# Feed-forward block of a streaming encoder layer: Strassen's seven products for eight, gate/up and down as two parts

## What is computed

```python
h = rms(x, ln1)
x = x + concat[SSD, HGRN2, FoX, RG-LRU](h @ w_in) @ w_out
h2 = rms(x, ln2)
x = x + (silu(h2 @ w_gate) * (h2 @ w_up)) @ w_down
```

## Time and profile before

| | |
|---|---|
| median of the runs shown | 2912.92 us |
| fastest run | 2911.31 us |
| profiled execution, span from first to last instruction | 2911.2 us |
| TensorE matmuls | 2832.2 us busy, 97% of the span |
| VectorE, ScalarE, GpSimd busy | 769.9, 820.2, 1010.4 us |
| phase 1 / w_out / feed-forward, by the trace | up to about 995 / 1199 / 2902 us |

### The profile page before, as it was taken

How to read it: one execution, slowest core, us unless ns; L and a number is a source line. 1 busy time by engine, 2 the same in 40 slices (tenths; PEclk the granted TensorE clock), 3 DMA queues, 4 the chain that set the end, 5 groups by cost and what they waited for, 6 DMA issues and landing times.

```text
span 2911.2 us, 47529 instructions
## 1 busy us (share of the span) xinstructions
PE 2832.2 (97%) x20795; PEld 2763.5 (95%) x20795; DVE 769.9 (26%) x1178; ACT 820.2 (28%) x1107; POOL 1010.4 (35%) x439
## 2 busy tenths in 40 slices
PE   5899999999999999999999999999999999999999
PEld 5899999988888999999999999999999999999998
DVE  6835444411125522311111111121111111111112
ACT  4333544443344522411212121211112121212121
POOL 3623222222223343333333333333333333333331
PEclk8999999999999999999999999999999999999999
DMA  6222222222223432323222222222232222222322
GB/s 196 75 74 75 68 66 79 68 71 71 71 56 117 126 94 80 87 76 84 87 73 88 78 83 88 73 87 85 76 88 84 77 87 73 87 78 83 87 79 89
DMA packets 372941, 244.86 MB, mean 84 GB/s; under 512 B 13024, under 2 KB 339916, under 8 KB 372172
## 3 DMA queue, kind: packets, MB, share of 16 engines
q1 hardware_dynamic: 356116, 228.55, 27.5%
q10 hardware_dynamic: 16632, 13.31, 1.5%
HBM read 225.40 MB, written 16.44 MB: 83 GB/s over the span
## 4 chain that ended last, share of the span: by engine, by line
PE 91%; DVE 6%; ACT 2%; issue 1%; DMA 0%; SPq 0%; ACTq 0%; POOL 0%; DVEq 0%
PE pair L546 89%; DVE scratch L1381 1%; ACT scratch L936 1%; DVE scratch L1373 1%; ACT L936 1%; DVE h_lo L1373 1%; DVE xtok L1381 1%; PE pair L755 1%; PE pair L577 0%; DVE scratch L1377 0%; DVE scratch L1378 0%; DMA xtok<-in_x_prompt_dram 0%; PE pair L922 0%; DVE y L1373 0%; DVE xT L1373 0%
## 5 line engine op out<-in xcount | busy, mean ns | idle before, releaser
L491 POOL TENSOR_TENSOR w_lo<-raw,w_hi 128x1024 fp32r<-128x1024 f32 x402 | 976.7, 2431 | 1852.7 <-ACT w_hi L936 1851.9
L546 PE MATMUL pair<-h_hi,w_hi 128*128 128x288 f32 x5024 | 1090.2, 299 | 33.7 <-DVE h_lo L1373 20.0
L546 PE MATMUL pair<-h_hi,w_lo 128*128 128x288 f32 x5024 | 1077.5, 296 | 0.0
L546 PE MATMUL pair<-h_lo,w_hi 128*128 128x288 f32 x5024 | 1077.3, 296 | 0.0
L546 PEld LDWEIGHTS pair<-h_hi,w_hi 128*128 128x128 f32 x5024 | 810.5, 189 | 43.6 <-issue 17.7
L546 PEld LDWEIGHTS pair<-h_lo,w_hi 128*128 128x128 f32 x5024 | 811.4, 189 | 0.0
L546 PEld LDWEIGHTS pair<-h_hi,w_lo 128*128 128x128 f32 x5024 | 811.3, 189 | 0.0
L936 ACT ACTIVATE w_hi<-raw 128x1024 fp32r<-128x1024 f32 x402 | 423.3, 1055 | 1017.5 <-PE pair L546 973.5
L546 PE MATMUL pair<-act_hi,w_hi 128*128 128x288 f32 x1408 | 304.7, 298 | 0.0
L546 PE MATMUL pair<-act_lo,w_hi 128*128 128x288 f32 x1408 | 302.6, 296 | 0.0
L546 PE MATMUL pair<-act_hi,w_lo 128*128 128x288 f32 x1408 | 302.6, 296 | 0.0
(11 more groups left out here) (179 smaller groups left out, 1102.6 us busy)
## 6 DMA issues: line engine op xcount, KB each, us to landing
raw<-in_w_in_dram SPq DMA_DIRECT2D x52, 1024.0 KB, 5.6
raw<-in_w_gate_dram SPq DMA_DIRECT2D x44, 1024.0 KB, 5.6
raw<-in_w_up_dram SPq DMA_DIRECT2D x44, 1024.0 KB, 5.6
raw<-in_w_down_dram SPq DMA_DIRECT2D x44, 1024.0 KB, 5.0
raw<-in_w_out_dram SPq DMA_DIRECT2D x16, 1024.0 KB, 6.0
xT_spill<-xT SPq DMA_DIRECT2D x4, 1152.0 KB, 10.1
xT<-xT_spill SPq DMA_DIRECT2D x4, 1152.0 KB, 10.5
xtok<-in_x_prompt_dram SPq DMA_DIRECT2D x4, 1024.0 KB, 7.4
```

The source lines that it names most:

```text
L491: pool.tensor_tensor(lo, src, hi.bitcast(F32), ALU.subtract).then_inc(S["lo_done"], 1)
L546: return nc.tensor.matmul(out, lhsT, rhs, start=start, stop=stop)
```

## The change

The feed-forward block is written anew with Strassen's scheme in Winograd's form. The matrices are cut in two along rows, along columns and along the tokens, and 7 products of quarters take the place of 8.

**Gate and up.** The weight quarters are gate and up of one feature tile for k-tiles 0 to 7 and for 8 to 15; the activation quarters are the token halves of the same k-tiles. A unit `u` is one feature tile, 44 of them (UG). Each of its 7 products is 8 k-tiles times 3 terms, 24 matmuls of 288 columns, all into one PSUM bank. The results are taken out of four banks (X, Y, Z, W) and added up on the way.

**Down.** The 44 tiles of the activations are 22 pairs, in 5 chunks of 5, 5, 4, 4, 4 pairs (CHUNK_PAIRS). A unit is two output tiles of one chunk, 8 units a chunk (UD), 40 in all. A product is 5 or 4 pairs times 3 terms: 15 or 12 matmuls.

**Weights.** VectorE makes four combinations of a unit's weight quarters (`combine`), each of 128 x 1024 for gate and up, 128 x 640 or 128 x 512 for down. ScalarE makes the seven `f_hi`. `f_lo` of products 0 and 5 is made by GpSimd (POOL_LO), of the other five by VectorE (DVE_LO). The buffers form a ring of three, `hi_ahead(s)` and `lo_ahead(s)` make those of product s+2 while product s runs. Weights are loaded two units ahead (`next_unit`).

**Activations.** The RMS factor is now applied before the split: `x_slot` on VectorE scales x by ln2 and `rstd2`, makes the four activation combinations and all seven `lo` within unit 0, and TensorE's product p of unit 0 waits for them (`in_lo`). Each even and odd unit's silu(gate) * up give a pair, GpSimd makes its four combinations (`combine_glu`), and SyncE writes the seven to DRAM (`spill_glu`, 5 DMAs). For each chunk of down the seven come back, one `load_stage` per product into two buffers `stage`, and are split again (`d_hi_slot` on ScalarE, `d_lo_slot` on VectorE) while the last unit of the chunk before runs.

**Residual.** x goes to DRAM tile by tile during w_out (`spill_x`) and comes back in 8 DMAs after the last gate/up product. The loops of the w_out and feed-forward phases are written out. Phase 1 keeps its instructions; some buffers lie at other addresses. The last 5 of 20 output transposes come after the last product, the other 15 between products of the last chunk.

```diff
+UG = FF // P
+CHUNK_PAIRS = (5, 5, 4, 4, 4)
+CHUNK_AT = (0, 5, 10, 14, 18)
+NC = len(CHUNK_PAIRS)
+UD = KT // 2
+U_ALL = UG + NC * UD
+LAST_C = U_ALL - UD
+PRODUCTS = 7 * U_ALL
+POOL_LO = (0, 5)
+DVE_LO = (1, 2, 3, 4, 6)
...
+            def next_unit(u):
+                sp.wait_ge(S["lo_by_pool"], 2 * u + 2)
+                sp.wait_ge(S["lo_by_dve"], 5 * u + 5)
+                if u + 2 < U_ALL:
+                    load_unit(u + 2)
...
+            def load_stage(c, p):
+                i, j0, n = 7 * c + p, CHUNK_AT[c], CHUNK_PAIRS[c]
+                sp.wait_ge(S["glu_spilled"], 80 * (j0 + n))
+                if i >= 2:
+                    sp.wait_ge(S["in_lo"], 14 + i - 1)
+                sp.dma_start(stage[i % 2][:, 0:n, :], glu_dram[j0:j0 + n, p].rearrange("j p n -> p j n")
+                             ).then_inc(S[f"stage{i % 2}_loaded"], 16)
...
+            for u in range(U_ALL):
+                c = chunk_after(u)
+                if c is None:
+                    next_unit(u)
+                else:
+                    for p in range(5):
+                        load_stage(c, p)
+                    next_unit(u)
+                    load_stage(c, 5)
+                    load_stage(c, 6)
+                if u < UG and u % 2 == 1:
+                    spill_glu(u // 2)
+                if u == UG - 1:
+                    sp.wait_ge(S["f_used"], 7 * UG)
+                    for m in range(KT // 2):
+                        sp.dma_start(xT[m // 4][:, 2 * m % 8:2 * m % 8 + 2, :],
+                                     xT_dram[2 * m:2 * m + 2].rearrange("k p t -> p k t")
+                                     ).then_inc(S[f"x_loaded{X_BACK[m][0]}"], 16)
...
+            def lo_ahead(s):
+                u, p = divmod(s + 2, 7)
+                if p in POOL_LO and u < U_ALL:
+                    pool.wait_ge(S["f_hi_done"], s + 3)
+                    slot = (s + 2) % 3
+                    pool.tensor_tensor(tiles(f_lo[slot], u), source(u, p), tiles(f_hi[slot], u).bitcast(F32),
+                                       ALU.subtract).then_inc(S["lo_by_pool"], 1)
...
+            for s in range(-2, PRODUCTS):
+                lo_ahead(s)
+                u, p = divmod(s, 7)
+                if p == 1 and 2 <= u <= UG and u % 2 == 0:
+                    combine_glu(u // 2 - 1)
...
-                            for r, (w, x) in enumerate(((wh, act_hi), (wh, act_lo), (wl, act_hi))):
-                                for b in range(2):
-                                    c0 = k * 2 * P + jj * P
-                                    m = mm(dst[:, b * 512:b * 512 + HT], w[:, c0:c0 + P],
-                                           x[:, k, b * HT:(b + 1) * HT], k == 0 and r == 0, k == 3 and r == 2)
...
+                if p == 4:
+                    pe.wait_ge(S["u_evac"], 5 * u + 2)
+                elif p == 5:
+                    pe.wait_ge(S["p1_ready"], u + 1)
+                elif p == 6:
+                    pe.wait_ge(S["u_evac"], 5 * u + 3)
...
+                wh, wl, dst = f_hi[s % 3], f_lo[s % 3], psum_of(u, BANK_OF[p])
+                for j in range(n):
+                    if u == 0 and j % 4 == 0:
+                        pe.wait_ge(S["in_lo"], 2 * p + j // 4 + 1)
+                    for q, (w, x) in enumerate(((wh, x_hi), (wh, x_lo), (wl, x_hi))):
+                        m = mm(dst, w[:, j * P:(j + 1) * P], x[:, j, :], p < 4 and j == 0 and q == 0,
+                               j == n - 1 and q == 2, skip_group_check=p > 3)
+                m.then_inc(S["f_used"], 1)
...
+            def hi_ahead(s):
+                u, p = divmod(s + 2, 7)
+                if u >= U_ALL:
+                    return
+                if p in (1, 2, 3, 4):
+                    act.wait_ge(S["s_made"], 4 * u + {1: 2, 2: 1, 3: 3, 4: 4}[p])
+                else:
+                    act.wait_ge(S[f"f_raw{u % 2}_loaded"], 32 * (u // 2 + 1))
+                if s + 2 >= 3:
+                    act.wait_ge(S["f_used"], s)
+                own.tell(fn(tiles(f_hi[(s + 2) % 3], u), source(u, p), ACT.Copy), "f_hi_done")
...
+            def d_hi_slot(c, p, u):
+                i, n = 7 * c + p, CHUNK_PAIRS[c]
+                act.wait_ge(S[f"stage{i % 2}_loaded"], 16 * (i // 2 + 1))
+                act.wait_ge(S["f_used"], 7 * u + p + 1)
+                own.tell(fn(dx_hi[p][:, 0:n, :], stage[i % 2][:, 0:n, :], ACT.Copy), "in_hi")
...
+                if which == 0:
+                    dve.wait_ge(S[f"f_raw{u % 2}_loaded"], 32 * (u // 2 + 1))
+                    own.tell(tt(source(u, 2), quadrant(u, 1, 0), quadrant(u, 1, 1), ALU.add), "s_made")
+                elif which == 1:
+                    dve.wait_ge(S["s_made"], 4 * u + 1)
+                    own.tell(tt(source(u, 1), source(u, 2), quadrant(u, 0, 0), ALU.subtract), "s_made")
+                elif which == 2:
+                    own.tell(tt(source(u, 3), quadrant(u, 0, 0), quadrant(u, 1, 0), ALU.subtract), "s_made")
+                else:
+                    dve.wait_ge(S["s_made"], 4 * u + 2)
+                    own.tell(tt(source(u, 4), quadrant(u, 0, 1), source(u, 1), ALU.subtract), "s_made")
+            def lo_ahead(s):
+                u, p = divmod(s + 2, 7)
+                if p in DVE_LO and 0 <= u < U_ALL:
+                    dve.wait_ge(S["f_hi_done"], s + 3)
+                    slot = (s + 2) % 3
+                    own.tell(tt(tiles(f_lo[slot], u), source(u, p), tiles(f_hi[slot], u).bitcast(F32), ALU.subtract),
+                             "lo_by_dve")
...
+            def x_slot(p):
+                t1, t2, t3 = gx_t[:, 4], gx_t[:, 0], gx_t[:, 3]
+                if p == 0:
+                    dve.wait_ge(S["rstd_ready"], 2)
+                    dve.wait_ge(S["xt_spilled"], 64 + 16 * KT)
+                    x_scaled(B11, 0)
+                    x_lo_slot(0, xq[:, B11])
+                elif p == 1:
+                    x_scaled(B12, 0)
+                    dve.wait_ge(S["x_made"], 16)
+                    x_combined(t1, xq[:, B12], xq[:, B11])
+                    x_scaled(B22, 8)
+                    dve.wait_ge(S["x_made"], 26)
+                    x_combined(t2, xq[:, B22], t1)
+                    x_lo_slot(1, t2)
...
+            def d_lo_slot(c, p):
+                i, n = 7 * c + p, CHUNK_PAIRS[c]
+                dve.wait_ge(S["in_hi"], 14 + i + 1)
+                own.tell(tt(dx_lo[p][:, 0:n, :], stage[i % 2][:, 0:n, :], dx_hi[p][:, 0:n, :].bitcast(F32), ALU.subtract),
+                         "in_lo")
+            def take(u, p, dst, x):
+                dve.wait_ge(S["f_used"], 7 * u + p + 1)
+                own.tell(tt(dst, x, psum_of(u, BANK_OF[p]), ALU.add), "u_evac")
...
+            def step(s):
+                if s > 0:
+                    u, p = divmod(s - 1, 7)
+                    evacuate_unit(u, p)
+                u, p = divmod(s, 7)
+                if p in (3, 4, 5):
+                    if u + 1 < U_ALL:
+                        combine(u + 1, p - 3)
+                elif p == 1:
+                    combine(u, 3)
+                lo_ahead(s)
+                if s > 0:
+                    u, p = divmod(s - 1, 7)
+                    if chunk_after(u) is not None:
+                        d_lo_slot(chunk_after(u), p)
...
```

More of the change, by code:

```diff
@@ L248, in hybrid_layer, with psum_of @@
+        def psum_of(u, which):
+            t = pair[2 * banks_of(u) + which // 2]
+            return t[:, 512 * (which % 2):512 * (which % 2) + HT]
+        X, Y, Z, W = range(4)
+        BANK_OF = (X, Y, Z, W, Z, X, W)
         C_BIAS, C_SGN, C_A, C_LS8, C_NLS8, C_LB, C_1MLB, C_NM, C_RS, C_RI, C_T, C_QN, C_SD = (
@@ L459, in _ @@
[L459 to L474 removed]
+            sp.wait_ge(S["norm_lo"], KT)
@@ L931, in _ @@
+            for c in range(5):
+                out_step(3, c)
         @block.scalar
@@ L1884, in _, with add_residual @@
-            swiglu(0, True)
-            with dve.Fori(1, GROUPS - 1) as g:
-                swiglu(g, False)
-            swiglu(GROUPS - 1, False, True)
+            def add_residual(k):
+                dve.wait_ge(S["half_used"], 2 * k + 2 * N1 + 2)
+                own.tell(tt(x_tile(k), x_tile(k), banks(pair[(k + 3) % 4]), ALU.add), "x2_done")
+                dve.wait_ge(S["x2_squared"], k + 1)
+                if k > 0:
+                    dve.wait_ge(S["x2_summed"], k)
+                own.tell(tt(ss2[:, :], ss2[:, :], sq2[k % 2][:, :], ALU.add), "x2_summed")
@@ new lines, in lo_ahead, with x_scaled @@
+            def lo_ahead(s):
[5 more added lines that the diff above has]
+                             "lo_by_dve")
+            def x_scaled(q, k0):
+                t = q in (B12, B22)
+                for j in range(8):
+                    own.tell(stt(xq[:, q, j, :], xq[:, q, j, :], pcol[:, R_LN2 + k0 + j:R_LN2 + k0 + j + 1],
+                                 rstd2[:, t * HT:(t + 1) * HT], ALU.mult, ALU.mult), "x_made")
@@ new lines, in x_combined, with x_lo_slot @@
+            def x_combined(dst, x, y):
```

(20 more changed lines are left out.)

528 lines of the change are left out of this document (295 added, 233 removed).

## The result

The changed kernel takes **2814.6 us** (median of 4 runs, 2812.48 to 2815.76) against 2912.1 for the kernel before in the same comparison (2909.11 to 2913.57). The ratio is 0.9664, with a 95% interval of 0.9650 to 0.9678: 97.5 us less, where 81 were forecast. The profiled execution has a span of 2813.1 us.

The account below looks back on a forecast made before the run. TensorE's matmuls were taken to bound the feed-forward block. Span 2911.2 - 210.9 - 12.0 + 41 + 3 + 19 + 6 + 56 + 8 + 7 + 1 = 2829.3 us; median 2831, range 2780 to 2890 (own range 2790 to 2865).

Parts of the forecast that it names:

- matmuls and group edges: Feed-forward block: 1584 fewer matmuls at 133.1 ns, 210.9 us less, and the loops' edge waits gone, 12.0 us less.
- unit 0, with its clock: First gate/up unit: VectorE's 56.5 us in one line delays TensorE, +41; last product perhaps at the lower clock, +3.
- units of 4 pairs, and the output copies: Down: VectorE sets the pace, 0.8 us too slow in 24 units, +19; output copies in the last 8, +6.
- changes of chunk, clock, x back: Five changes: loads and seven extra low parts, +56; lower clock while TensorE is half idle, +8; x reload, +7.
- end: After the last product: take, addition, then five transposes and stores; 9.0 us before, +1.
- Gate/up: Units 1 to 42: 22.4 us each, latencies covered by two products ahead, cost 0.
- slower rival: Gate/up: GpSimd and VectorE shut each other out; gain gone from 24.5 us a unit, 2961 at 25.5; 6 in 100.
- The 8 us for the clock: Chunk changes: TensorE half idle for some 25 us each time, so clock granted at 0.67; +8, 0 to 20.
- x back: Start of down: x reload of 4.7 MB delays product 4 of unit 44 and unit 46's weights; +7, 0 to 20.
- Down is fed in time: Rival, down: VectorE's 93% share is enough and loads are prompt; without 19, 56, 8 and 7, 2741 us; 8 in 100.
- VectorE bound throughout down: Rival, down: each GpSimd operation holds VectorE in full, in units and at changes; 2877 us; 17 in 100.

## Why the prediction was right, and where it was not

The gain was forecast as 82 us of span and is 98. By the prediction's own terms (measured: from the start of w_out's last matmul, 1186.8 us before and 1188.6 after, to the last product, and from there to the end):

| term | forecast | measured |
|---|---|---|
| matmuls and group edges | -222.9 | -238.0 |
| unit 0, with its clock | +44 | +44.7 |
| units of 4 pairs, and the output copies | +25 | +8.7 |
| changes of chunk, clock, x back | +71 | +85.2 |
| end | +1 | -0.5 |
| start of the block | 0 | +1.8 |
| sum | -81.9 | -98.1 |

In part the total is near by luck: the first and the third term came out 15 and 16 us better than forecast, and the changes of chunk took 14 of these back.

In the kernel before the feed-forward block begins at 1187.0 us, not near 1199, where the table of phases puts the end of w_out. In its first 96 matmuls TensorE waits once, at the half, and the sum over partitions stands behind them:

```profile
1193.89 0.51 PE L546 MATMUL pair<-h_hi,w_hi 128*128 128x288 f32 x2 [0.35 <-DVE h_lo L1381]
1200.36 1.13 PE L546 MATMUL pair<-ss,ones 128*128 128x288 f32 x4
```

Counted back from either, and from the last product too (12672 matmuls), the first one starts at 1187.0. The last w_out addition at 1190.77 comes late because VectorE was still making eight `h_lo`.

**Matmuls removed.** Before, 1715.4 us lie between the two points; fed, 44 x 22.40 + 16 x 14.00 + 24 x 11.16 = 1477.4 lie there now. 133.3 ns a matmul, as the row had it: up to 24 in a row into one bank cost nothing, which had been the condition. An estimate by the figure of the Trainium skill, TensorE: Matmul & The Clock Gate, "Wait — 56ns, not 53.3ns?" (122.5 ns here) has gate/up at 20.6 us a unit; the trace does not bear it out. The 1584 matmuls are 211 of the 238 us. The edges were sized too small, at 12.0 us from the one row of waits: the starts of the matmuls before leave 19 gaps of over 0.4 us, together 20.6 us beyond a matmul each, and 45 shorter ones with 4.9 us. Ten of the 19 are not waits at a group's edge: there TensorE makes output transposes, which take some 5 us in all and had one wait of 1.7 us. The changed kernel has to make them too, so these 5 us come back two terms below.

**Gate/up.** Right: 22.40 us a unit, no stall, with the cover of two products ahead that the text named. The slower rival did not come about, though its mechanism did: both engines are held (2730 ns for 2431), by 0.3 us and not by what it needed.

**Unit 0.** Right in size: from w_out's end to unit 1, 67.1 us against 66.4. VectorE is busy for 59.25 of them, so it is the bound as said, and GpSimd's part in it is 3 us, by the run without it.

**Units of 4 pairs: the step that failed on the good side.** The prediction: "VectorE sets the pace, 0.8 too slow: 24 units, +19". They run at 11.16, fed. The holds were real; VectorE's timeline and the group in the changed kernel, 2510 to 2570 us:

```profile
2518.61 0.68 DVE L1535 TENSOR_TENSOR f_lo<-s_buf,f_hi 128x512 fp32r<-128x512 f32 x1
2519.22 0.68 DVE L1535 TENSOR_TENSOR s_buf<-f_raw,s_buf 128x512 f32<-128x512 f32 x1
2519.82 0.68 DVE L1535 TENSOR_TENSOR f_lo<-f_raw,f_hi 128x512 fp32r<-128x512 f32 x1
2520.42 0.45 DVE L1535 TENSOR_TENSOR pre<-pre,pair 128x288 f32<-128x288 f32 x1
```

```profile
L1535 DVE TENSOR_TENSOR xT_half<-xT_half,glu 128x288 f32<-128x288 f32 x5 | 6.7, 1350 | 0.2
L1535 DVE TENSOR_TENSOR xT_half<-xT_half,up 128x288 f32<-128x288 f32 x11 | 5.0, 458 | 0.4
```

The addition of `glu` takes 1350 ns, 0.9 held, where 0.8 was the estimate; in the kernel whose GpSimd makes no low parts it takes 458. What was wrong is the price of operations in a row: one lasts 0.68 us, yet the next starts after 0.60, so 0.08 us of each lie under the next. The prediction took 0.02, from eight `h_lo` in 5.92 us held against 758 ns, which is the duration of another kind of operation (a single `h_lo` at 1192.94 lasts 0.81, which gives 0.08 here too). With 18 operations in a unit that is 1.1 us, more than the 0.8 that were missing. In the window of five such units VectorE is busy for 50.69 of 55.80 us, 91%, with all holds: 10.1 us a unit instead of 11.9. The last seven units take 86.8 for 78.1, 8.7 more. The output copies on VectorE, forecast at 6, are not the main part of it: TensorE is busy for 85.88 us there, with 648 matmuls where 588 belong to products. The other 60 are output transposes, and by the starts of the matmuls they take 5.5 us. The sum had them in no term. At most 3.2 us are left for the copies.

**Changes of chunk: the term that was mis-sized.** 56 + 8 + 7 forecast, 85.2 measured. The mechanism (VectorE's seven extra low parts and the loads in front of them) is the one at work, and the ends that the text gave are found: 25 for "loads are prompt and only VectorE's own excess counts" over five changes, 28.9 measured over the last four. The other 38.5 of their 67.4 us went with the loads made early; moving x and GpSimd's share, which that kernel has too, were worth 1.4 and 1.1 us in these four by themselves. The landings were estimated at 4.2 and 3.6 us and are 6.9 and 5.1; and the first load comes not promptly but behind 1.3 MB of weights, which kept ScalarE 4.79 us and VectorE 5.66. The 8 us for the clock are a cost that isn't there in the four changes where the run filled idle time with matmuls. "x back" was 7 forecast; putting x ahead of the stores was worth 7.5.

**Rivals.** "Down is fed in time" fell on the changes alone, "VectorE bound throughout down" on the units of 4 and 5 pairs, which are fed.
